# Hyena branch: where the gate's loads and the merge's first loads stand in their queues

## The reference

```
def long_conv(u, hf, bias):
    uf = jnp.fft.rfft(u, n=2 * seqlen, axis=1)
    y = jnp.fft.irfft(uf * hf[None], n=2 * seqlen, axis=1)[:, :seqlen]
    return y + u * bias

z = x1 * long_conv(v, hf[:, 0], bias[0])
z = x2 * long_conv(z, hf[:, 1], bias[1])
return z * jax.nn.silu(p['z_b'])
```

## Time and profile before

| | us |
|---|---|
| median of 3 runs | 4280.57 (4278.86 to 4286.88) |
| the profiled execution, its own time | 4274.1 |
| its span | 4272.2 |
| TensorE busy | 4088.2 (96%) |
| VectorE busy | 2790.6 (65%) |
| GpSimd busy | 1895.5 (44%) |
| ScalarE busy | 1211.0 (28%) |
| mean granted TensorE clock | 0.981 of full speed |

### The profile page before, as it was taken

One profiled execution on the slowest core, in us unless ns is written; L12 is line 12 of the kernel. 1 busy time (PEld: TensorE's weight loads), 2 busy tenths in 40 slices (PEclk: granted clock), 3 DMA queues, 4 the chain that ended last, 5 costly groups with the idle time before them and its releaser, 6 DMA issues. The chain is left out here.

```text
span 4272.2 us, 74646 instructions
## 1 busy us (share of the span) xinstructions
PE 4088.2 (96%) x29523; PEld 2554.8 (60%) x29523; DVE 2790.6 (65%) x4228; ACT 1211.0 (28%) x2579; POOL 1895.5 (44%) x1498
## 2 busy tenths in 40 slices
PE   6999999999999999999988999989999997999998
PEld 3455544444444444444437888866666655887887
DVE  5667754532457868896726666657777766678765
ACT  4112111111211211111114555555555553010000
POOL 1322333332233343433339999935455444444432
PEclk8999999999999999999999999999999998999999
DMA  8233222223243332425347888747687876745642
GB/s 290 68 93 106 85 84 85 79 99 106 84 164 102 105 117 79 123 79 159 103 149 208 214 257 254 212 122 227 215 250 220 235 238 217 240 152 189 208 134 77
DMA packets 519332, 665.17 MB, mean 156 GB/s; under 512 B 122048, under 2 KB 412808, under 8 KB 508364
## 3 DMA queue, kind: packets, MB, share of 16 engines
q1 hardware_dynamic: 472090, 530.36, 40.7%
q0 software_dynamic: 26448, 104.86, 7.7%
q10 hardware_dynamic: 20450, 25.17, 1.7%
HBM read 442.75 MB, written 217.53 MB: 155 GB/s over the span
## 5 line engine op out<-in xcount | busy, mean ns | idle before, releaser
L1534 PE MATMUL proj_b<-shared_S,proj_tw 128*128 128x512 f32 x1920 | 848.1, 593 | 0.0
L1534 PEld LDWEIGHTS proj_b<-shared_S,proj_tw 128*128 128x128 f32 x1920 | 360.5, 190 | 432.6 <-issue 431.9
L1534 PE MATMUL proj_b<-shared_A,shared_wt 128*128 128x512 f32 x1280 | 576.9, 593 | 7.2 <-PEq L159 6.7
L863 POOL TENSOR_TENSOR proj_tw<-shared_wt 128x512 f32<-128x512 f32 x80 | 115.9, 1449 | 883.6 <-PE proj_b L1534 822.6
L1534 PEld LDWEIGHTS proj_b<-shared_A,shared_wt 128*128 128x128 f32 x1280 | 243.6, 190 | 311.5 <-issue 311.0
L1534 PE MATMUL proj_b<-shared_A,proj_tw 128*128 128x512 f32 x640 | 287.9, 592 | 3.1 <-DVE proj_u L1176 3.1
L1534 PE MATMUL proj_b<-shared_S,shared_wt 128*128 128x512 f32 x640 | 290.1, 596 | 0.0
L1898 DVE SCALAR_TENSOR_TENSOR delta_la<-delta_kkq,bridge_region,delta_wm 128x256 f32<-128x256 f32 (+1 forms) x288 | 121.6, 464 | 174.8 <-PE delta_kkq L1998 174.8
L1079 ACT ACTIVATE proj_v<-proj_b 128x512 f32<-128x512 f32 x80 | 47.8, 597 | 662.4 <-PE proj_b L1534 662.4
L1171 DVE TENSOR_TENSOR proj_u<-proj_b,proj_u 128x512 f32<-128x512 f32 x80 | 55.3, 691 | 274.8 <-PE proj_b L1534 274.7
L1534 PEld LDWEIGHTS proj_b<-shared_A,proj_tw 128*128 128x128 f32 x640 | 121.4, 190 | 156.8 <-issue 149.9
(11 more groups left out here) (409 smaller groups left out, 9160.6 us busy)
## 6 DMA issues: line engine op xcount, KB each, us to landing
shared_wt<-in_w_in_dram POOLq DMA_DIRECT2D x80, 1024.0 KB, 6.1
scratch_bounce_f<-tail_first SPq DMA_DIRECT2D x128, 256.0 KB, 4.4
bridge_region<-scratch_bounce_f SPq DMA_DIRECT2D x32, 1024.0 KB, 7.6
scratch_bounce_i<-fft_yi SPq DMA_DIRECT2D x64, 512.0 KB, 3.4
fft_second<-scratch_bounce_i SPq DMA_DIRECT2D x32, 1024.0 KB, 8.6
scratch_hy<-shared_hA SPq DMA_DIRECT2D x48, 512.0 KB, 2.6
delta_ring<-scratch_NV SPq DMA_DIRECT2D x96, 256.0 KB, 4.1
delta_ring<-scratch_KQ SPq DMA_DIRECT2D x88, 256.0 KB, 4.3
```

The lines of the kernel that those rows point to most:

```text
L863: pool.tensor_tensor(T3, w[:, hi, second], w[:, lo, second], ALU.subtract).then_inc(combined, 1)
L1534: last = pe.matmul(bank[:, :], weights[:, k, :], aa[operand][:, k, :], start=(k == 0), stop=(k == KH - 1))
```

## The change

SP's gate loads become a function of their own, called in the loop over h behind the first inverse write and filter_read(t, 2). On POOL, merge_weights waits for D 15 of the last step, no longer for A 15 of the last step (the end of its filter stage, which comes before its data transforms).

```diff
@@ -2199,6 +2199,14 @@
+                def gate_loads(t):
+                    cb, o = t // 2, t % 2
+                    wait(sp, z_done, PAIR * t)
+                    for b in range(2):
+                        src = T["hy"][KT + 2 * cb + b] if o == 0 else T["zb"][2 * cb + b]
+                        for e in range(2):
+                            sp.dma_start(ga[64 * e:64 * e + 64, b, :, :], src[e:N1:2, :, :]).then_inc(ga_in, 16)
+
@@ -2221,11 +2229,6 @@
                         sp.wait_ge(y_stored, 16 * cb)
-                    wait(sp, z_done, PAIR * t)
-                    for b in range(2):
-                        src = T["hy"][KT + 2 * cb + b] if o == 0 else T["zb"][2 * cb + b]
-                        for e in range(2):
-                            sp.dma_start(ga[64 * e:64 * e + 64, b, :, :], src[e:N1:2, :, :]).then_inc(ga_in, 16)
                     wait(sp, gated, 3 * t)
@@ -2240,6 +2243,8 @@
                         if h in (0, 2):
                             filter_read(t, h // 2 + 2)
+                        if h == 0:
+                            gate_loads(t)
@@ -2402,7 +2407,7 @@
                 def merge_weights():
                     last = STEPS - 1
-                    ready(pool, "A", last, N2 - 1)
+                    ready(pool, "D", last, N2 - 1)
```

## The result

| | before | after |
|---|---|---|
| median | 4280.57 | 4373.32 (4368.54 to 4374.12, 4 runs) |
| profiled execution | 4274.1 (span 4272.2) | 4374.1 (span 4372.2) |

The ratio on record is 1.0222, 95% interval 1.0210 to 1.0234; the medians lie 92.8 us apart. The forecast was 4366.6. The two profiled executions lie 100.0 us apart; 4.3 of these arose before Hyena's first row of SP (2817.24 and 2821.56, where nothing was changed) and are scatter.

A forecast was written before the change was run, and what follows sets the result against it. TensorE, busy 96% of the span, bounds the kernel, so only its holes matter. 85 - 6 + 16 - 9 = +86 us on the median 4280.57 gives 4366.6, range 4320 to 4400.

The forecast's parts named there:

- part 1: SP's gate loads behind the first inverse write and third filter read: 12.2 us a step lost, +85, less 6 gained.
- The landing of the gates: Gate loads land 17.2 us after a step's first inverse write is issued (T); bounds 13 and 20; step 7: 19.2.
- the moment at which the sums are wanted: POOL's sums for the next step wanted 29.9 us after the first inverse write's issue, 37.0 with the write stall.
- credit of 6: First inverse write and third filter read no longer behind gates: 1.3 us in step 6, 4.9 in steps 2, 4; -6.
- part 2: Heads and weights (4 MB, POOL's queue) behind D of step 7: the 7.2 us TensorE hole closes, -9, at least 7.
- The write stall: Second inverse write lands behind the gate loads in SP's queue; ACT's inverse(3) waits for it, 7.1 us a step.
- Rival B: Transfers overlap: second inverse write passes the gates, which land at their lower bound; no write stall; +48, 4328; chance 0.19.
- The filter stage's hole: POOL's sums come 7.1 us late; less 3.0 of reserve, 4.1 us a step opens in TensorE's filter stage.
- the reserve with the clock behind it: Filter stage: 3.0 us before DVE's shape(3) is delayed, less 1 us a step (0 to 3) for low-clock matmuls.
- rival D: Dearer: clock losses not absorbed (3 us a step more) and issue holes return in every step; +115, 4396; chance 0.13.
- The 4.9 us of issue holes: TensorE waits called issue in steps 2 and 4, of 6.1 us in all, forecast to vanish; part of the -6.
- The end of step 7: Gates 24.1 us later, outputs(7) 22.2 later; DVE without waiting -2, heads ready -4: +16 where Z transposes go on.

The follow-up runs named there:

- experiment 3: The whole change, but POOL issues the four gate loads on its own queue at the same moment: 4369.45 us, ratio 1.0218.
- experiment 7: The whole change, but the gate loads stand one h later, behind the second inverse write instead of the first: 4385.66 us, ratio 1.0248.
- 10: The kernel before with one more wait, holding POOL's gating back about as late as in the change, all DMAs untouched: 4385.08 us, ratio 1.0251.
- Experiment 4: The whole change, with POOL's third gating operation (times the norm) cut to 1 of its 16 parts: 4320.05 us, ratio 1.0098.
- experiment 1: The kernel before with only merge_weights changed, heads and weights behind D of the last step: 4270.51 us, ratio 0.9984.
- experiment 9: The whole change, but only two of four gate loads are late; the other two are issued as in the kernel before: 4338.92 us, ratio 1.0143.

## Why the prediction was right, and where it was off

- **The sum of part 1** was to be 85 us for steps 0 to 6, less 6. Measured from the profiled executions: write 0 of step 0 to write 0 of step 7 takes 753.3 us instead of 670.9, and with the closed hole of 9.9 that makes 92.3, against the 79 forecast.
- **The landing of the gates**, T + 17.2, was measured (by the start of gating) at T + 17.0 to 18.7, 0.8 later on the mean. That costs 6 us. Against it stands the moment at which the sums are wanted: T + 29.9 is step 5's, and the mean of steps 0 to 6 is T + 31.3, which takes 10 off; for these the forecast had its credit of 6 (below). Together 2 of the 13 us missing. In step 7, 19.2 was forecast and 17.1 came: write 0 took 4.9 us there, 1.4 more than in step 5. That need not be the 4 MB of part 2, for in step 1 it took 4.9 as well.
- **The write stall** was forecast at 7.1 and is 7.5 in step 5, 5.5 on the mean of the waits (1.3 in step 6). The size was about right and the ground was only half right: I let the order in SP's queue decide. In the kernel after, order is what one sees, but experiment 3 shows that much the same comes from another queue. Rival B, in which write 1 overtakes, did not happen; the write was 15.3 us under way.
- **The filter stage's hole**: 4.1 forecast, 29.3 / 7 = 4.2 measured. That both delays make one maximum was the prediction's "whatever the first one's part is", and experiments 7 and 10 show it.
- **The step that failed** is the reserve with the clock behind it, a term mis-sized: 3.0 us of reserve less 1 us for slow matmuls, so 2 us a step in TensorE's favour. Measured, the part of a step behind the start of the sums is 62.8 against 63.2 before: 0.4. That is 11 of the 13 us missing. The reserve is there, but the slow matmuls eat it. The view of windows shows this, from the start of the sums to the next T (length, then busy times; PEclk is the third column from the end), steps 2 and 4 before, then steps 2 and 4 after:

```profile
3096.64:3158.83 62.19, 60.61 (x601) 42.70 (x594) 45.49 (x66) 32.47 (x55) 20.35 (x17) 1.00 0.89 250
3286.08:3347.77 61.69, 60.37 (x598) 42.52 (x590) 45.49 (x66) 32.48 (x55) 21.41 (x17) 1.00 0.90 252
```

```profile
3138.30:3197.99 59.69, 55.40 (x529) 39.63 (x526) 42.13 (x60) 30.97 (x51) 19.75 (x17) 1.00 0.72 204
3352.97:3415.26 62.29, 56.47 (x509) 39.77 (x506) 42.30 (x60) 30.80 (x51) 19.70 (x17) 0.95 0.68 185
```

In step 2 the clock stayed full, and the stretch is 2.5 us shorter than before; in step 4 it was 0.95, and nothing is left. Over the seven steps it is 0.95, 0.97, 1.00, 0.97, 0.95, 0.97 and 0.94, a mean of 0.964. If TensorE worked at half speed in the missing part, that is 62.8 x 0.036 = 2.3 us of work a step, an estimate from these rows, where the forecast had 1. Experiment 4, which takes the second holes away, agrees: it gave back 9 us more than their length, 8 at the end and the 7 that I had put for the clock. In this point rival D was right by half.
- **A row misread.** "8 matmuls in 3.78 us where 16 take 3.6" is true of L2635 (16 in 3.62 at 3503.39), but rows 11 do not show it: their second line is 16 smaller transposes behind a hole of 9.0 us.
- **The 4.9 us of issue holes** in steps 2 and 4 were to vanish. They did not; 6.8 us of such holes are in the kernel after, mostly in other steps. But they lie within POOL's time now and cost nothing, and so does what made the sums begin later than T + 29.9 before. So the credit of 6 came, as 10, and not for the reason given.
- **Part 2**: -9 for the hole (at least 7); experiment 1 shows step 6 shorter by 9.9 and the end longer by 1.2.
- **The end of step 7**: +16 forecast, 86.4 - 71.2 = +15.2 measured; outputs(7) began at 3690.90 = T + 59.8 (forecast after T + 58; the sum had 40.3 + 22.2 = 62.5). So they began 2.7 us earlier than in the sum, and what follows gained 4.3 us instead of the 6 of the sum; the two errors partly cancel.

Between the profiled executions the miss is 14 us: 13 in steps 0 to 6, -1 for the hole, -1 at the end, and 2 by which write 0 of step 0 came later without a cause in the change. Between the medians it is 7, because the profiled execution of the kernel before lay 6.5 us under its median. So half of the closeness is scatter; the mechanism is the one forecast.

## What to carry to other kernels

Before a load is moved behind other transfers, look for the longest serial work that begins with its landing (here 26.9 us of POOL and then the next stage's sums) and count its reserve from the timeline: here POOL had none in step 6 and 6.0 us at most (step 0). Most of a delay beyond it was lost in each step: experiment 9, with the gates 4.8 us earlier than in the change, gained 3.9 a step. Two late things that run side by side cost their maximum here; removing the more visible one (the write stall, experiment 7) gave back nothing. A transfer that an engine with two buffers waits for should not meet 2 MB of large packets, whichever of the two queues they stand in; of this change only part 2 is worth keeping, 4270.51 us, 0.16% under the kernel before.

## What the runs showed of the hardware that I had not expected

Beside a queue of 7 KB packets a queue of 1 KB packets got 12 to 19% of the DMA engines' time, though about as many packets were served of each (experiment 3); the 512 KB write took 13.9 us instead of 3.5 to 5, nearly as long as behind the same loads in one queue (15.3). And after a hole of 7.5 us the same 8 transposes took 1.97 us instead of 1.09; the granted clock of 3427 to 3437 in the kernel after is 0.66 of full speed, so 1.2 GHz instead of 2.4 for part of it. It does not follow every hole: behind the filter stage's holes of 3.0, 3.5 and 3.6 us (steps 2, 1 and 5) the 8 transposes took 1.10 us, behind those of 4.2 us and more 1.98. The view of windows:

```profile
3427.00:3437.00 10.00, 2.51 (x30) 1.60 (x12) 1.54 (x3) 2.22 (x5) 3.43 (x1) 0.66 0.96 286
```

Why TensorE waited at "issue", and why in other steps than before, was not tried.
